# Down projection of a ConvFFN: eight of 22 contraction tiles as seven half-size products per pair of output tiles

## The reference

```
x = x + merged @ w_o
h2 = rmsnorm(x, g_ffn)
f_gate, f_up = split(h2 @ w_up)                 # each 520 x 2816
x = x + (silu(causal_conv3(f_gate)) * f_up) @ w_down     # 2816 -> 1024
y = rmsnorm(x, g_final)
```

## Time and profile before

| | |
|---|---|
| Median of 3 runs | 844.01 us (844.00 to 844.06) |
| Span of the profiled execution | 842.0 us |
| TensorE busy | 832.4 us, 99% |
| VectorE busy | 680.6 us, 81% |
| ScalarE busy | 418.2 us, 50% |
| GpSimd busy | 128.8 us, 15%, none in the down projection |
| Down projection, first to last matmul | 707.6 to 835.0 us |
| Behind the last matmul | 7.0 us |

### The profile page before, as it was taken

One profiled execution on the slowest core, in us unless ns is written; L12 is line 12 of the kernel. 1 busy time (PEld: TensorE's weight loads), 2 busy tenths in 40 slices (PEclk: granted clock), 3 DMA queues, 4 the chain that ended last, 5 costly groups with the idle time before them and its releaser, 6 DMA issues.

```text
span 842.0 us, 18330 instructions
## 1 busy us (share of the span) xinstructions
PE 832.4 (99%) x6896; PEld 829.0 (98%) x6896; DVE 680.6 (81%) x1026; ACT 418.2 (50%) x754; POOL 128.8 (15%) x98
## 2 busy tenths in 40 slices
PE   8999999999999999999999999999999999999996
PEld 7999999999999999999999999999999999999996
DVE  4899898999999966766569899989999998544343
ACT  7753636464332234663235666546655658232232
POOL 2283838466000000000002300000000000000000
PEclk9999999999999999999999999999999999999999
DMA  9424232432332343327732133333342334444423
GB/s 262 126 79 119 81 95 83 148 110 81 100 116 85 91 112 90 87 75 125 178 98 76 50 86 111 91 104 112 102 123 82 108 110 119 108 114 103 104 66 115
DMA packets 190457, 88.93 MB, mean 106 GB/s; under 512 B 36472, under 2 KB 188940, under 8 KB 190372
## 3 DMA queue, kind: packets, MB, share of 16 engines
q1 hardware_dynamic: 186225, 86.29, 36.6%
q10 hardware_dynamic: 4171, 1.82, 0.8%
HBM read 83.79 MB, written 3.51 MB: 104 GB/s over the span
## 4 chain that ended last, share of the span: by engine, by line
PE 98%; DVE 1%; ACT 0%; issue 0%; ACTq 0%; DVEq 0%
PE psum L1862 44%; PE psum L1868 22%; PE psum L2032 14%; PE psum L2037 7%; PE psum L2060 4%; PE psum L2065 2%; PE psum L2181 1%; PE psum L2190 1%; PE psum L1905 1%; PE psum L1840 1%; PE psum L1903 1%; PE psum L1912 0%; PE psum L1977 0%; DVE w_lo L1446 0%; PE psum L1950 0%
## 5 line engine op out<-in xcount | busy, mean ns | idle before, releaser
L1862 PE MATMUL psum<-act,w_hi 128*128 128x260 f32 x2600 | 341.0, 282 | 0.0
L1862 PEld LDWEIGHTS psum<-act,w_hi 128*128 128x128 f32 x2600 | 323.0, 188 | 0.0
L1148 DVE TENSOR_TENSOR w_lo<-raw,w_hi 128x1024 fp32r<-128x1024 f32 (+2 forms) x110 | 129.9, 1183 | 77.1 <-ACT w_hi L586 76.7
L1868 PE MATMUL psum<-act,w_lo 128*128 128x260 f32 x1300 | 185.1, 282 | 0.0
L1868 PEld LDWEIGHTS psum<-act,w_lo 128*128 128x128 f32 x1300 | 168.2, 188 | 0.0
L586 ACT ACTIVATE w_hi<-raw 128x1024 fp32r<-128x1024 f32 (+2 forms) x110 | 107.0, 976 | 87.7 <-PE psum L1868 85.1
L554 POOL TENSOR_TENSOR gate_a<-gate_a,prods 128x512 f32<-128x512 f32 x72 | 110.0, 1527 | 79.7 <-ACT prods L671 71.3
L2032 PE MATMUL psum<-act,w_hi 128*128 128x260 f32 x576 | 91.2, 282 | 0.7 <-ACT tmp L935 0.7
L2032 PEld LDWEIGHTS psum<-act,w_hi 128*128 128x128 f32 x576 | 78.8, 188 | 0.9 <-ACT tmp L935 0.9
L2032 PE MATMUL psum<-mid,w_hi 128*128 128x260 f32 x432 | 68.5, 282 | 0.0
L1225 DVE SCALAR_TENSOR_TENSOR psum<-u,cst,psum 128x512 f32<-128x512 f32 x96 | 66.8, 745 | 0.0
(11 more groups left out here) (215 smaller groups left out, 1003.0 us busy)
## 6 DMA issues: line engine op xcount, KB each, us to landing
raw<-in_w_in SPq DMA_DIRECT2D x56, 512.0 KB, 3.7
raw<-in_w_up SPq DMA_DIRECT2D x44, 512.0 KB, 3.8
raw<-in_w_down SPq DMA_DIRECT2D x16, 384.0 KB, 3.8
raw<-in_w_down SPq DMA_DIRECT2D x16, 320.0 KB, 3.1
v<-in_x_prompt SPq DMA_DIRECT2D x8, 512.0 KB, 6.4
raw<-in_w_b_out SPq DMA_DIRECT2D x8, 512.0 KB, 3.7
raw<-in_w_a_out SPq DMA_DIRECT2D x8, 512.0 KB, 5.1
raw<-in_w_o SPq DMA_DIRECT2D x8, 512.0 KB, 4.2
```

The source lines that it names most:

```text
L1148: ve.tensor_tensor(w_lo[:, slot, 0:k, :], raw[:, s, 0:k, :], w_hi[:, slot, 0:k, :], ALU.subtract).then_inc(lo_done, 1)
L1862: pe.matmul(a[:, h, :], w_hi[:, s, j, :], rhs(k, part)[:, h * H:(h + 1) * H], start=start and part == 0, stop=False)
L1868: last = pe.matmul(a[:, h, :], w_lo[:, s, j, :], rhs(k, 0)[:, h * H:(h + 1) * H], start=False, stop=stop)
```

## The change

The down projection becomes twelve jobs in the order p0 p1 p2 s0 p3 s1 p4 s2 p5 s3 p6 p7.

- A plain job p_j does the first 14 contraction tiles of output tile j: two weight units of 7 tiles, 14 x 6 = 84 matmuls.
- A seven job s_m does the last 8 contraction tiles of the output tiles 2m and 2m + 1 together: seven products of 12 matmuls. Its P4 is done inside the plain job behind it, after 12 of that job's matmuls.
- The token sums of the last 8 tiles (16 differences of 128x260, and their hi and lo parts) are made by VectorE and ScalarE during p0 and p1; hi and lo parts of these activation tiles are made there too. They lie in memory that was free or is dead by then.
- Every seven job needs the four weight sums, as in the up projection. Its snapshots and bank contents are added into `xT` by VectorE (`add_snaps`, `add_5`, `add_22`, `add_zy`, `add_21`), and so is the plain job's (`plain_out`).
- `y_block`, `move_y`, `y_square` and `y_scale` of a tile come when both its jobs are done. The loops are unrolled. The last output tile is p7: still in two parts of columns, with 14 contraction tiles each.

The core of the diff:

```diff
+    DOWN = [(kind == "s", int(j)) for kind, j in ("p0", "p1", "p2", "s0", "p3", "s1", "p4", "s2", "p5", "s3", "p6", "p7")]
...
+            def load_down(n):
+                seven, j = DOWN[n - FT]
+                for half, which in enumerate(("gate", "up")):
+                    s = raw_at(n, which)
+                    sp.wait_ge(q_lo, raw_free(n - 2, which))
...
+            for n in range(FT, JOBS):
+                load_down(n)
+                for j in {JOB_P[4]: (0, 1), JOB_P[5]: (2, 3), JOB_P[6]: (4,), JOB_P[7]: (5, 6)}.get(n, ()):
+                    move_y(j)
...
+            def step_of_p(n):                       # ScalarE
+                if n > FT:
+                    hi_up(n)
+                if n + 1 < JOBS:
+                    if SEVEN[n + 1]:
+                        hi_2(n + 1)
+                    hi_open(n + 1)
+            def step_of_s(n, squares):
+                hi_4(n)
+                up_1(n)
+                for j in squares[:1]:
+                    y_square(j)
+                hi_3(n)
+                hi_open(n + 1)
+                up_v(n)
+                up_5(n)
+                for j in squares[1:]:
+                    y_square(j)
...
+            step_of_s(JOB_S[0], ())
...
+            step_of_s(JOB_S[1], (0, 1))
+            step_of_p(JOB_P[4])
+            step_of_s(JOB_S[2], (2, 3))
+            step_of_p(JOB_P[5])
+            step_of_s(JOB_S[3], (4,))
+            hi_up(JOB_P[6])
+            y_square(5)
+            hi_open(JOB_P[7])
+            hi_up(JOB_P[7])
+            y_square(6)
...
+            def step_of_p(m, blocks, scales):       # VectorE
+                n = JOB_S[m] - 1
+                if m > 0:
+                    add_zy(m - 1)
+                else:
+                    plain_out(1)
+                weight_sum_1(n + 1)
+                lo_up(n)
+                if m > 0:
+                    add_21(m - 1)
+                weight_sum_2(n + 1)
+                weight_sum_3(n + 1)
+                for j in blocks[:1]:
+                    y_block(j)
+                lo_2(n + 1)
+                lo_open(n + 1)
+                weight_sum_4(n + 1)
+                for j in scales:
+                    y_scale(j)
+                for j in blocks[1:]:
+                    y_block(j)
+            def step_of_s(m, scales):
+                plain_out(m + 2)
+                lo_4(n)
+                lo_3(n)
+                add_snaps(m)
+                lo_open(n + 1)
+                for j in scales:
+                    y_scale(j)
+                add_5(m)
+                add_22(m)
...
+            down_sums(0)
+            down_sums(1)
+            x_times_root(1)
+            down_token_lo(0)
+            lo_open(JOB_P[1])
+            down_sums(2)
+            plain_out(0)
+            lo_up(JOB_P[1])
+            down_token_lo(1)
+            down_sums(3)
+            x_times_root(2)
+            down_token_lo(2)
+            lo_open(JOB_P[2])
+            down_token_lo(3)
+            step_of_p(0, (), ())
+            step_of_s(0, ())
...
+            step_of_p(1, (0, 1), ())
+            step_of_s(1, (0,))
...
+            step_of_s(3, (4,))
+            y_block(5)
+            add_zy(3)
+            lo_up(JOB_P[6])
+            add_21(3)
+            lo_open(JOB_P[7])
+            y_scale(5)
+            plain_out(6)
+            lo_up(JOB_P[7])
+            y_block(6)
...
+            def down_seven(m):                      # TensorE
+                product("P1", n)
+                pe.wait_ge(c1_set, NTH[n])
+                product("P2", n)
+                pe.wait_ge(snap, 3 * NTH[n] + 1)
+                product("P6", n)
+                product("P5", n)
+                pe.wait_ge(snap, 3 * NTH[n] + 2)
+                product("P7", n)
+                pe.wait_ge(snap, 3 * NTH[n] + 3)
+                product("P3", n)
```

More of the change, by code:

```diff
@@ L2031, in hi @@
                     for part in range(2):
-                        pe.matmul(bank, w_hi[:, slot, k, :], b_part(b, part, j), start=opens and j == 0 and part == 0, stop=False,
+                        pe.matmul(bank, w_hi[:, slot, k, :], home(b, part, j), start=opens and j == 0 and part == 0, stop=False,
                                   skip_group_check=not opens)
@@ L2150, in turn_tail_f @@
                     pe.transpose(psum[0:n, 4, j * P:(j + 1) * P], tail[:, c:c + n], ident[:, :]).then_inc(f_turned, 1)
-            def down(n, par):
-                for s in range(RING):
-                    unit(G_DOWN + RING * n + s, s, in_down, t=G_DOWN + n, dst=par, slot=DOWN_SLOT[s],
-                         ks=range(KFIRST[s], KFIRST[s] + KSPLIT[s]), first=s == 0, final=s == RING - 1,
-                         done=tiles_from(S_G))
-            pe.wait_ge(cx_set, FT)
-            pe.wait_ge(prod_done, START + 2 * KT + FT - 1)
@@ L2162, in _, with down_plain, hi, lo @@
-            down(0, 0)
-            turn_tail_f()
-            with pe.Fori(0, KT // 2 - 1) as it:
-                for par in range(2):
-                    down(2 * it + 1 + par, 1 - par)
+            def down_plain(j):
+                n, a = JOB_P[j], down_banks(j)
+                for c, (slot, g) in enumerate(((1, "gate"), (3, "up"))):
+                    pe.wait_ge(q_hi, HI[g, n])
+                    def hi(at):
+                        k = KC * c + at
+                        if j == 0:
+                            pe.wait_ge(act_lo, START + S_G + k + 1)
+                        for part in range(2):
+                            for h in range(2):
+                                pe.matmul(a[:, h, :], w_hi[:, slot, at, :], in_down(k, part)[:, h * H:(h + 1) * H],
+                                          start=k == 0 and part == 0, stop=False)
+                    def lo(at):
+                        k = KC * c + at
+                        for h in range(2):
+                            last = pe.matmul(a[:, h, :], w_lo[:, slot, at, :], in_down(k, 0)[:, h * H:(h + 1) * H], start=False,
+                                             stop=k == KD - 1)
+                        return last
+                    for at in range(KC - 1):
+                        if c == 0 and at == 3 and SEVEN[n - 1]:
+                            fourth(n - 1)
+                        hi(at)
+                    pe.wait_ge(q_lo, LO[g, n])
+                    for at in range(KC - 1):
+                        lo(at)
+                    hi(KC - 1)
+                    lo(KC - 1).then_inc(p_done, 1)
@@ L2168, in turn_last @@
+            down_plain(6)
             def turn_last(tiles):
@@ L2187, in _ @@
                         turn_last(LAST_TILES[0])
-                    pe.wait_ge(lo_done, g + 1)
-                    for j in range(KSPLIT[s]):
-                        last = pe.matmul(last_acc(part), w_lo[:, DOWN_SLOT[s], j, :], in_down(KFIRST[s] + j, 0)[:, lo:hi], start=False,
-                                         stop=s == RING - 1 and j == KSPLIT[s] - 1)
+                    pe.wait_ge(q_lo, LO[g, JOB_P[KT - 1]])
+                    for at in range(KC):
+                        last = pe.matmul(last_acc(part), w_lo[:, slot, at, :], in_down(KC * c + at, 0)[:, lo:hi], start=False,
+                                         stop=c == 1 and at == KC - 1)
                 last.then_inc(last_part, 1)
```

404 lines of the change are left out of this document (272 added, 132 removed).

## The result

| | before | after |
|---|---|---|
| Median of 4 runs each, same session | 844.03 us (844.00 to 844.18) | 856.41 us (854.62 to 857.42) |
| Span of the profiled execution | 842.0 us | 853.6 us (own time 855.95) |
| p0 begins on TensorE | 707.62 | 709.69 |
| T, the last output tile begins | 818.68 | 830.85 |
| from T to the end | 23.3 us | 22.75 us |

The ratio is 1.0142, 95% interval [1.0128, 1.0157]: slower, as forecast, but by 12.4 us where 7.7 were forecast, and 0.4 us above the upper end of the range. The runs of after also scatter over 2.8 us, those of before over 0.2.

What follows compares the result with a forecast made beforehand. TensorE, busy for 832.4 of 842.0 us, was taken as the bound, with the end set by tile 6's move. 842.0 + 0.9 + 6.5 + 0.3 = 849.7 us of span, plus 2.0 gives 851.7; range 845.5 to 856.

Steps and rivals of the forecast that it cites:

- Part 4: In s1, s2, s3 TensorE waits ahead of P7, behind `y_square` waiting for its move: 1.4, then about 2.5 each, sum 6.5 us.
- the walk: Stepping through the written instruction lists of ScalarE and VectorE from 700.3 us, each instruction with its step, to time the stalls.
- Part 1: Down projection matmuls go from 1056 to 1008: 48 fewer at 0.120 us, 5.8 us, all behind T.
- part 5: At the end tile 6's move and chain, not matmuls, set the time: the whole matmul saving given back, and 0.3 us more.
- The rival in which the end follows TensorE: At the second L1784: the last tile's 48 matmuls count in full, 5.9 us, so 838 to 839 with no stall; chance 0.05.
- the weights are there some 4.4 us into the next plain job: For s2 and s3, weights issued behind two moves arrive at 4.4 us, are wanted at 3.4; everything shifts by 1.0 us.
- with no stall the last tile starts at the same moment: 924 matmuls stand before p7 as before the old last tile, so T stays 818.68.
- Part 3: Token sums on VectorE at the start: p2's first weight unit 0.2 late, s0's opening weights 0.7, together 0.9 us of stall.
- the main case: Stalls in all three later seven jobs and the end bound by tile 6's move; likeliest 851.7 us, chance 0.67.
- slower steps of SP: SP issuing at the loop's 0.82 us a step: the stalls in s1 to s3 sum to about 10 us.

Runs made afterwards that it cites:

- Experiment 4: The changed kernel with both squares of a seven job behind its last snapshot (`up_5`) instead of one ahead of `hi_3`; 851.11 us, ratio 1.0092.
- experiment 5: The changed kernel with `y_block(6)` directly behind `plain_out(6)`, then `lo_up` of p7, then `y_scale(5)`; 855.23 us, ratio 1.0135.
- experiment 6: The changed kernel with the last move (tile 6) issued half by SP and half by ScalarE; 854.27 us, ratio 1.0118.
- experiment 1: The kernel before with the changed kernel's memory layout alone: 14,560 B per partition behind `ones`, DMA scratch space 1 KB; 846.24 us, ratio 1.0022.
- experiment 2: The kernel before with the DMA scratch space cut to 1 KB and nothing else; 844.25 us, ratio 0.9999.
- experiment 3: The kernel before with the changed kernel's memory layout, plus a 32-byte gap behind `t_more`; 844.30 us, ratio 1.0.
- experiment 10: The changed kernel with all order and queue edits of kernel 9 together, but without its 32-byte gap; 844.60 us, ratio 1.0004.
- experiment 7: The changed kernel with `lo_open` of p2 ahead of `down_token_lo(2)` on VectorE; 856.09 us, ratio 1.0136.
- experiment 8: The changed kernel with a 32-byte gap behind `t_more`, nothing else; 853.18 us, ratio 1.0104.
- Kernel 9: The changed kernel with squares later, one move ahead of weights, `y_scale` later, tile 6's blocks first, its move on two queues, p2's weights first, 32-byte gap; 842.30 us.
- experiment 11: Kernel 9 with VectorE's residual sum for TensorE's last transposes ahead of the scaling of row group 3; 842.39 us, ratio 0.9976.

## Why the prediction was right and wrong

The sum of the prediction against the two spans, in us more than before:

| term | forecast | measured |
|---|---|---|
| from the start to p0 (not edited) | 0 | 2.1 |
| waits at p2 and s0 | 0.9 | 1.5 |
| waits ahead of P7 in s1, s2, s3 | 1.4, 2.5, 2.5 (summed as 6.5) | 1.6, 1.3, 3.2 (6.1) |
| half clock behind s3's wait | 0 | 1.5 |
| rest up to T | 0 | 1.0 |
| T to the end | +0.3 | -0.55 |
| span | +7.7 | +11.6 |
| own time above the span | 2.0 | 2.35 |

A measured wait is what the trace shows as idle and 0.16 for the refill: the first matmul behind a wait takes its whole 0.28, the others come at a pace of 0.12. Of the last 1.0 before T, 0.2 are s3's opening weights; the rest is not assigned.

**The sign and its cause: right.** Part 4 was the term that decides, and it was: TensorE waited three times ahead of P7, for `up_v`, behind a square that waited for its move. Experiment 4 takes the squares away and the waits are gone. In s1, where nothing else was late, the walk gave 1.4 and the trace 1.48.

**Part 1 and part 5: right.** All 48 matmuls went behind T and were given back there. Experiments 5 and 6 show what held the end: shorten tile 6's chain by 1.3 or 1.9 and the time falls by 1.2 or 2.1. The rival in which the end follows TensorE is refuted by the 5.2 us for which TensorE waits for L2039. One detail of part 5 was wrong: `y_scale(5)` did not hold `plain_out(6)`. It was over at 830.6, and `plain_out(6)` started at T + 0.2, not T + 1.5. TensorE's slow stretch behind s3's wait had pushed T back while the others worked on: tile 5's square began at 826.25, T - 4.6, where the walk had T - 2.9. That is most of why the end got 0.55 us shorter instead of 0.3 longer.

**Part 4's two later waits: sizes wrong, both ways.** The step that failed is "the weights are there some 4.4 us into the next plain job", for s2 and s3 alike. For s2 they were in use 5.8 us after the first issue and 3.6 into p4 (776.11 - 772.55), near what was wanted, and that wait was 1.3. For s3 they were there only 8.1 us after the issue, 5.8 into p5 (799.87 - 794.07), and the wait was 3.2. I had taken one landing time for both. The second time one part in sixteen of each load came 2.0 and 2.2 us behind the others, beside a 16 KB packet of kind "instruction"; the sum had no term for that. By an estimate from the two waits (3.2 against 1.3) it stands behind 1.9 us of s3's wait, and so behind its being the one that was long enough to cost the clock.

**The first missing term: the layout, 2.1 us.** This is the step of the sum that failed most: it put the start up to p0 at nothing without a reason ("with no stall the last tile starts at the same moment"). The diff adds a tile ahead of the activations, and the sum had no line for what that does to the 700 us that are not edited. Experiments 1 to 3 show that it costs 1.9 us, by the pace of the matmuls, and experiment 10 that it costs 2.3 in the best order. This was the largest error of the sum.

**The second missing term: the clock, 1.5 us.** The sum priced a wait at its length. The longest one also cost the clock behind it. It is so in all five profiles in which the last wait ahead of P7 is 2.6 us or more, those of after and of experiments 5 to 8, and in none of experiments 4, 9, 10 and 11, whose waits ahead of T are all under 1 us. It was not tried by itself. It also bears on the scatter: each execution has its mean granted clock on record, and of after's four the slowest (857.42) has the lowest, 0.990, and the fastest (854.62) the highest, 0.995. In experiment 7 the two at 0.990 took 857.34 and 857.88, the two at 0.995 and 0.994 took 854.84 and 854.81; in experiment 4 the slowest (854.65) is the one with the lowest, 0.992. Not all of it follows: one run of after took 856.88 at 0.994. Kernel 9's runs lie within 0.4 us, at 0.996 and 0.997.

**Part 3: right in kind, too low.** p2 0.2 and s0 0.7 were forecast; the trace has 0.8 and 0.4, and the refill. I had walked VectorE's list with steps from isolated groups, and experiment 7 shows how full it is: a wait taken away in p2 came back in s0.

The upper end of the range, 856.0, was the main case with slower steps of SP. It held no term for the unchanged part and none for the clock; either would have taken the measured 856.41 in.

## What to carry to other kernels

An instruction that waits for a DMA belongs behind the last thing on its engine that TensorE waits for; here one loop line moved was worth 5.3 us. Matmuls saved in the last tile are worth next to nothing while the chain beside them sets the end: shorten that chain in the same change, as kernel 9 does, or expect the saving back. And when a change adds a tile, look at where the tiles behind it come to lie, and compare the pace of matmuls in a stretch that was not edited before anything else.

## What the runs showed of the hardware

- **Activation tiles moved by 14,560 bytes in the partition slowed TensorE's pace, moved by 14,592 bytes they did not**, with fp32r matmuls of 260 columns: 1417 matmuls against 1424 in 170 us of the input projection (0.5%), at granted clock 1.00 and never idle. Of the whole it was 1.9 and 2.3 us in two pairs of kernels; in a third p0 began 1.7 us later. Which of the moved tiles does it, and whether it is TensorE's own reads or what the other engines do to the same tiles, was not tried.
- **The granted clock fell to 0.50 behind waits of 2.6 to 3.0 us**, in all five profiles that have one (after and experiments 5 to 8), 2.0 to 4.3 us after TensorE had stopped, twice before it had started again. It stayed there for 3.4 us in four of them and for 6.8 in experiment 7. It stayed at 1.00 behind the waits of 1.1 to 1.5 us of the same runs. In after the cost was about 1.5 us on top of the wait.
- **SP issued the eight DMAs of a move at 0.70 us each** when written out (834.32 to 839.26 is seven steps), so a move of one output tile keeps its queue for 5.6 us, and whatever is queued behind it comes later by that.
- **One part in sixteen of a weight load came 1.4 to 2.4 us behind the others**, in the four profiles of after and of experiments 6, 7 and 8, each time with a 16 KB packet of kind "instruction" in flight beside the load (in after from 793.83, for 2.30 us).
